# A two-block transformer on one core: how TensorE's moving operand is laid out and read, and where the weight tiles stand

## The reference, cut to what matters

```
h = rmsnorm(x, g_mix);           z = h @ w_in
x = x + (gc*conv_branch + ga*attn_branch) @ w_mix_out
x = x + square(relu(rmsnorm(x, g_mlp) @ w_ff1)) @ w_ff2
...
x = x + gate_m * (concat([attn, ssm]) @ w_out)
x = x + gate_f * conv_ffn(h, w_up, conv_w, conv_b, w_down)
```

## Time and profile before

| | |
|---|---|
| runs, median (lowest to highest) | 2446.01 us (2444.16 to 2446.15) |
| span of the profiled execution | 2444.7 us |
| TensorE matmul busy | 2423.8 us, 99% |
| weight loads busy (beside the matmuls) | 2149.2 us, 88% |
| VectorE busy | 1969.0 us, 81% |
| ScalarE busy | 1261.4 us, 52% |
| DMA | 566.81 MB, mean 232 GB/s |

### The profile page before, as it was taken

One profiled execution on the slowest core, in us unless ns is written; L12 is line 12 of the kernel. 1 busy time (PEld: TensorE's weight loads), 2 busy tenths in 40 slices (PEclk: granted clock), 3 DMA queues, 4 the chain that ended last, 5 costly groups with the idle time before them and its releaser, 6 DMA issues.

```text
span 2444.7 us, 47745 instructions
## 1 busy us (share of the span) xinstructions
PE 2423.8 (99%) x14373; PEld 2149.2 (88%) x14373; DVE 1969.0 (81%) x3114; ACT 1261.4 (52%) x2038; POOL 89.1 (4%) x109
## 2 busy tenths in 40 slices
PE   8999999999999999999999999999999999999998
PEld 7888888888888888888888988889888888888887
DVE  7778876689987887887898877776887887887886
ACT  6444445565554454554555555565545445445455
POOL 0000001000000000000000105300000000000000
PEclk9999999999999999999999999999999999999999
DMA  7786885657888888888888555555566656656555
GB/s 275 274 282 211 279 284 192 200 190 268 285 292 293 287 291 292 286 293 291 289 288 281 175 177 194 188 171 190 167 187 200 202 180 198 198 178 212 192 176 169
DMA packets 162812, 566.81 MB, mean 232 GB/s; under 512 B 18883, under 2 KB 19452, under 8 KB 162748
## 3 DMA queue, kind: packets, MB, share of 16 engines
q1 hardware_dynamic: 132572, 458.71, 56.4%
q10 hardware_dynamic: 27792, 101.20, 12.5%
q0 software_dynamic: 2384, 6.09, 1.0%
HBM read 563.51 MB, written 2.42 MB: 231 GB/s over the span
## 4 chain that ended last, share of the span: by engine, by line
PE 77%; DVE 4%; issue 2%; ACT 1%; DVEq 0%; DMA 0%; ACTq 0%; SPq 0%
PE bank L334 77%; DVE w_lo L1345 1%; DVE scratch L1994 0%; DVE scratch L1992 0%; DVE scratch L1351 0%; DVE scratch L1997 0%; ACT w_hi L823 0%; DMA w_raw<-in_w_in 0%; DVE Z L1705 0%; DVE H L1714 0%; DVE scratch L2020 0%; ACT U L1297 0%; DVE scratch L2014 0%; DVE scratch L1378 0%; PE bank L678 0%
## 5 line engine op out<-in xcount | busy, mean ns | idle before, releaser
L1345 DVE TENSOR_TENSOR w_lo<-w_raw,w_hi 128x1024 fp32r<-128x1024 f32 (+2 forms) x898 | 1048.0, 1176 | 117.1 <-ACT w_hi L823 107.5
L334 PE MATMUL bank<-H,w_hi 128*128 128x512 f32 (+1 forms) x4480 | 1100.0, 386 | 9.3 <-ACT w_hi L275 8.1
L334 PEld LDWEIGHTS bank<-H,w_hi 128*128 128x128 f32 x4480 | 799.3, 188 | 136.7 <-issue 11.2
L823 ACT ACTIVATE w_hi<-w_raw 128x1024 fp32r<-128x1024 f32 (+2 forms) x898 | 876.4, 1012 | 24.1 <-PE bank L334 8.4
L334 PEld LDWEIGHTS bank<-H,w_lo 128*128 128x128 f32 x4416 | 591.5, 188 | 40.5
L334 PE MATMUL bank<-H,w_lo 128*128 128x256 f32 x4416 | 602.9, 277 | 0.0
L334 PE MATMUL bank<-U,w_hi 128*128 128x512 f32 (+1 forms) x2011 | 501.7, 384 | 0.5 <-DVE U L2022 0.3
L853 ACT ACTIVATE scratch<-bank 128x256 f32<-128x256 f32 x355 | 135.1, 381 | 669.3 <-PE bank L334 668.7
L334 PEld LDWEIGHTS bank<-U,w_hi 128*128 128x128 f32 x2011 | 351.1, 188 | 50.0 <-DVE U L2022 0.6
L334 PEld LDWEIGHTS bank<-U,w_lo 128*128 128x128 f32 x1984 | 275.3, 188 | 23.7
L334 PE MATMUL bank<-U,w_lo 128*128 128x256 f32 x1984 | 282.1, 277 | 0.0
(11 more groups left out here) (246 smaller groups left out, 1113.2 us busy)
## 6 DMA issues: line engine op xcount, KB each, us to landing
w_raw<-in_w_ff SPq DMA_DIRECT2D x256, 512.0 KB, 5.0
ada_w<-in_w_ada ACTq DMA_DIRECT2D x192, 512.0 KB, 4.7
w_raw<-in_w_up SPq DMA_DIRECT2D x176, 512.0 KB, 4.5
w_raw<-in_w_z SPq DMA_DIRECT2D x96, 512.0 KB, 4.8
w_raw<-in_w_in SPq DMA_DIRECT2D x88, 512.0 KB, 4.4
w_raw<-in_w_gate SPq DMA_DIRECT2D x64, 512.0 KB, 4.6
w_raw<-in_w_down SPq DMA_DIRECT2D x64, 384.0 KB, 3.2
w_raw<-in_w_down SPq DMA_DIRECT2D x64, 320.0 KB, 3.4
```

Source lines behind the costliest of these rows:

```text
L334: return nc.tensor.matmul(out, lhsT, rhs, start=start, stop=stop, skip_group_check=True)
L823: A(w_hi[:, slot, 0:cols], w_raw[:, slot, 0:cols], ACT.Copy).then_inc(sem("w_high"), 1)
L1345: TT(w_lo[:, slot, 0:cols], w_raw[:, slot, 0:cols], w_hi[:, slot, 0:cols].bitcast(F32), ALU.subtract)\
```

## The change

`H`, `U` and `B` become plain contiguous chunks, with no threading. The matmul reads such a chunk in four rounds: lines 0, 4, 8, ..., then 1, 5, 9, ..., then 2, 6, ... and 3, 7, .... The output is addressed in the same turn, so that each result lands where it did. VectorE and ScalarE write and read the chunks through the same kind of view as before, whose lines now adjoin. The two weight tiles get an offset in front: 11 lines for `w_hi`, 10 for `w_lo`. Counted to the areas of the moving operand modulo 16 lines they now stand 9 and 14 lines off. `U`, `B` start 1024 elements further on and coincide with `G` and `Z`; in the gap behind `H` stand `R` and `ss`.

```
-STEP = 3
 LINES = 2 * T // LINE
-CHAIN_N = NC * 2 * T + (STEP - 1) * 2 * T
+AREA_N = NC * 2 * T
+GAP = 1024
+MOVING_AT, HIGH_AT, LOW_AT = 0, 11, 10
...
-            area = nc.alloc_sbuf_tensor_at(name, [P, CHAIN_N], F32R, offset=base + at)
-            return bass.AP(area[:, :].tensor, LINE, [[CHAIN_N, P], [2 * T, NC], [STEP * LINE, LINES], [1, LINE]])
+            area = nc.alloc_sbuf_tensor_at(name, [P, AREA_N], F32R, offset=base + 4 * at)
+            return area[:, :].rearrange("p (k l e) -> p k l e", k=NC, e=LINE)
...
-        U = chunks_by_line("U", NC * 2 * T * 4)
-        B = chunks_by_line("B", 2 * NC * 2 * T * 4)
+        U = chunks_by_line("U", AREA_N + GAP)
+        B = chunks_by_line("B", 2 * AREA_N + GAP)
...
-        w_hi = sb("w_hi", [P, 4, PIECE], F32R)
-        w_lo = sb("w_lo", [P, 4, PIECE], F32R)
+        w_hi, w_lo = (sb(name, [P, LINE * at + 4 * PIECE], F32R)[:, LINE * at:].rearrange("p (s c) -> p s c", s=4)
+                      for name, at in (("w_hi", HIGH_AT), ("w_lo", LOW_AT)))
...
-        R = sb("R", [P, T])
-        ss = sb("ss", [P, T])
+        R = nc.alloc_sbuf_tensor_at("R", [P, T], F32, offset=base + 4 * AREA_N)
+        ss = nc.alloc_sbuf_tensor_at("ss", [P, T], F32, offset=base + 4 * (AREA_N + T))
...
+        def in_turn_of_lines(ap):
+            return ap.rearrange("p (i a) e -> p a i e", a=4)
...
             def mm_lines(out, lhsT, rhs, start, stop):
-                return mm(lines(out), lhsT, rhs, start, stop)
+                return mm(in_turn_of_lines(lines(out)), lhsT, in_turn_of_lines(rhs), start, stop)
```

More of the change, by code:

```diff
@@ L106, in build @@
     with ExitStack() as ctx:
-        base = (nc.sbuf_base + 31) // 32 * 32
-        ctx.enter_context(nc.sbuf_tensor("arena", [P, 3 * NC * 2 * T + 1024 + (Z_BLOCKS - 32) * T], F32))
+        base = (nc.sbuf_base + 31) // 32 * 32 + 4 * LINE * MOVING_AT
+        ctx.enter_context(nc.sbuf_tensor("arena", [P, LINE * MOVING_AT + 3 * AREA_N + GAP + (Z_BLOCKS - 32) * T], F32))
         def sb(name, shape, dt=F32):
@@ L121, in chunks_by_line @@
         def chunks_by_line(name, at):
-            area = nc.alloc_sbuf_tensor_at(name, [P, CHAIN_N], F32R, offset=base + at)
-            return bass.AP(area[:, :].tensor, LINE, [[CHAIN_N, P], [2 * T, NC], [STEP * LINE, LINES], [1, LINE]])
+            area = nc.alloc_sbuf_tensor_at(name, [P, AREA_N], F32R, offset=base + 4 * at)
+            return area[:, :].rearrange("p (k l e) -> p k l e", k=NC, e=LINE)
         H = chunks_by_line("H", 0)
-        U = chunks_by_line("U", NC * 2 * T * 4)
-        B = chunks_by_line("B", 2 * NC * 2 * T * 4)
-        G = nc.alloc_sbuf_tensor_at("G", [P, NC, 2, T], F32, offset=base + NC * 2 * T * 4 + 4096)
-        Z = nc.alloc_sbuf_tensor_at("Z", [P, Z_BLOCKS, T], F32, offset=base + 2 * NC * 2 * T * 4 + 4096)
+        U = chunks_by_line("U", AREA_N + GAP)
+        B = chunks_by_line("B", 2 * AREA_N + GAP)
+        G = nc.alloc_sbuf_tensor_at("G", [P, NC, 2, T], F32, offset=base + 4 * (AREA_N + GAP))
+        Z = nc.alloc_sbuf_tensor_at("Z", [P, Z_BLOCKS, T], F32, offset=base + 4 * (2 * AREA_N + GAP))
         X = sb("X", [P, NC, T])
```

## The result

The changed kernel takes 2460.43 us (median of four runs, 2459.34 to 2461.97) against 2445.09 us before (median of four, the three runs named above and one more): 1.0063 times as long, 95% interval 1.0052 to 1.0075, 15.3 us more. 2384.5 had been forecast, with 0.26 for slower. The time lies inside the stated range, 2341 to 2480, but that range covers both signs, and the kernel became slower where a gain had been forecast. It is a small difference: 0.6%, clear of the spread of the runs.

What follows compares the result with a forecast made beforehand. TensorE's matmuls were taken to bound the kernel; 8.4 ns from reading order plus 0.5 from offsets, over 6912 couples, gave 61.5 us less, 2383.2 of span and 2384.5 us. The range was 2341 to 2480, the forecast's own 2360 to 2425.

Steps and rivals of the forecast that it cites:

- The bound: Whole kernel: TensorE's matmuls, busy 2423.8 of 2444.7 us, set the end, so their gain arrives in full.
- Offsets of the weight tiles: Weight tiles: moving them acts on 2.2 ns of stall a couple; 0.5 ns gain taken, ends all gone or doubled.
- The split of the stalls: Each high and low couple: 14.9 ns of stalls, about 12.6 from the moving stream, 2.2 from meeting the weight load.
- the narrow products: Matmuls of `H` with 16- or 32-column weights: 3 ns slower than full tiles, so place counts; should fall some 5 ns.
- The sign named in the prediction: PE timeline: high and low matmuls shrink in ratio of columns if the moving stream causes it, low alone if offsets.
- Order of reading: Moving operand: going from steps of three lines to four removes two thirds of 12.6 ns, 8.4 ns a couple.
- a larger step must be better: Moving operand: adjoining lines are the worst order and larger steps better, from step 1 up to 260 ns, step 3 at 225.
- The row of contiguous reading: Four matmuls of `wn` by `wn`, read line after line: 260 ns each, taken as an end and not a price.
- The other terms, at nothing: Results written in turn, ScalarE and VectorE access to `H`, `U`, `B`, and new addresses: each forecast to cost nothing.
- The size of the stalls: All matmuls: 339.1 ns a couple against a floor of 324.2, 14.9 ns of stalls, 103 us or 4.2% in all.
- Collisions come back: Rival, every matmul: rounds stay on one residue modulo four and meet the weight load; 31 us slower, 2477, chance 0.19.
- Results: Rival, PSUM writes: jumps between groups of four results cost 20 ns a couple, 139 us; time 2524, chance 0.07.

Runs made afterwards that it cites:

- the scan: Programs of matmuls alone, on zeros, varying reading order and weight-tile distances, later all 16 x 16 pairs: 2666 to 2795 ns in rounds, 2707 to 2787 in steps of three.
- 14, 1: Changed kernel with weight tiles at 14 (high) and 1 (low) lines behind the moving area modulo 16: 2424.26 us, 0.9914 of the kernel before.
- rounds_7_7: Changed kernel with the low tile moved from 2 to 7 lines behind the moving area modulo 16, high left at 7: 2446.96 us, 1.0007.

## Why the prediction was wrong

**The bound** was read rightly: TensorE's pace went to the end almost one for one (PE +14.4 us, span +13.7), no engine and no load became late, and counts, writers of the areas and queues cost nothing.

**The step that failed in sign is "Offsets of the weight tiles".** I gave them 0.5 ns of gain a couple, out of 2.2 ns that I thought was all they could touch, with "it doubles" as the bad end. They cost 22 us at four rounds (2460.4 against 2438.5), which is 3.2 ns a couple over 6912, more than the bad end. Two errors led there. The split of the stalls took the second half of a high matmul, when no weights are being read, as the moving stream's own cost. But by the positions' rows a stall isn't local: the same matmul takes 219 or 231 ns by its place in the row, so how a matmul goes hangs on those before it. And the row that told otherwise stood in the prediction: the narrow products, 3 ns slower with next to no weights to load, "so the place of the weights counts". It went into the price of a rival, and into the sum not at all. The sign named in the prediction, low matmuls alone for the offsets, points the same way: eight low ones lost 16 ns and eight high ones, with twice the columns, 10.

**The step that failed in size is "Order of reading"**, and more of the missing time is its: 8.4 ns a couple forecast, 1.0 measured at equal distances (6.7 us / 6912). Of the 76 us between forecast and time some 51 are this term, some 25 the offsets. It rested on the same split, which gave 12.6 ns to the moving stream, and on the argument that a larger step must be better, which falls with eight rounds at 1.93 us and more. The row of contiguous reading was also misread: 260 ns is the mean of three steps of which the first follows a wait. Taken one by one, the starts in the same trace are 315, 233 and 236 ns apart, and the scan has 229 to 234. The other terms, at nothing, held.

**The size of the stalls**, 103 us above the floor, was tested by no run. The floor comes from the transposes, read as free of stalls, so that "the transposes run at exactly that floor" was no argument for it. The kernel with the least of them that I found still stands well above: at 14, 1 a couple takes on average 336 ns, (2698 + 2675)/16, against 324.

**The rivals.** "Collisions come back" was the nearest, with weights and moving operand at a bad distance and too high a price: 31 us against the 22 that the distance costs, and nothing for what the order gains. It had 0.19. Its mechanism, rounds that stay on one residue modulo four, isn't borne out: the same change of place costs steps of three 29 us, and they stay on no residue. What spoke against it, "the distance of the new layout is the same for all", was no comfort: a constant distance can be constantly bad. "Results" is excluded. On writing: "PSUM — Partial Sum Buffer" (Specifications) of the Trainium skill would have any non-contiguous access slow matmuls significantly; the two pairs of kernels with and without groups of four results 16 elements apart contradict it, 2444.9 with them for 2445.1 without, and 2460.4 with them for 2461.0 without. "Advanced Engine Details and Errata" (PSUM Cachelines) of the Trainium skill repeats that rule and adds that every two neighbours should be contiguous; the runs fit the addition. And "TensorE: Matmul & The Clock Gate" (Step-by-step) of the Trainium skill says that a weight load takes no read bandwidth from the running matmul; here moving only the weight tiles changed the kernel's time by 36 us (2424.3 to 2460.4), so for these float32r matmuls the measurement decides against the rule as the prediction used it, that the place of the weights can't matter.

**What a better reading would have been.** This is hindsight. The kernel before had all wide matmuls alike to 1 or 2 ns, while its narrow products, at other distances, varied from 222 to 232. That could have warned that its tiles stood in a favourable place, and that a move of them was a draw with unknown outcome, not a small gain: of the 256 pairs in steps of three, the scan found none better than the one it had.

**What stays open.** Why the period is 16 lines. That memory is divided into sixteen parts by line, and that two streams in one part stall each other, would fit it and the bad steps of eight, but no run shows the parts; it is a guess. Nor is it shown what at a seam sets which row the pieces behind it fall into, or whether the small differences of a few nanoseconds between two kernels are enough for it.

## What to carry to other kernels

When float32r matmuls, each with a weight tile of its own, follow each other without a gap, the place of the weight tile relative to the moving operand, modulo 256 bytes, is a tuning knob worth 1.5 to 1.7% here (2424 to 2460 us in rounds, 2445 to 2487 in steps of three). It has to be swept in the kernel itself together with the order of reading: a loop of matmuls alone ranks settings only roughly, all the more if it is short. If a change alters both the order and the place, measure them apart before judging either. Count the distance from the first element that is really read: one line of start in the view was enough to mislead here. And judge by starts of single matmuls by position, since means and busy time hide a pattern of 219 to 240 ns.

## What the runs showed of the hardware that was not expected

- The pace of float32r matmuls repeats with the distance of weights and moving operand at 16 lines of 16 bytes, in all five orders, but for three distances in four rounds; between best and worst distance lie 3% in four rounds (2701 to 2781 ns).
- A step of eight lines costs 7% against four (1.93 to 2.01 us for eight of 512 columns, against 1.79 to 1.85).
- Groups of four results 16 elements apart in PSUM cost nothing (2444.9 us against 2445.1, and 2460.4 against 2461.0).
- At one pair of distances matmuls have more than one steady pace, and keep it for a hundred microseconds or more: in `rounds_7_7` 1813 ns for eight high from 196 to 242 us and 1801 and 1766 in turn from 251 to 354; in the changed kernel 2740 ns for eight couples in most stages and 2713 in the mixing stage.
- At one and the same seam, a stretch of short products with waits, the granted clock was 0.80 on the mean of 17 us before and 0.90 after; the same matmuls took 1.4 us less.
